# Scaling the last tile's rows on GpSimd, with the third placement and the last count moved, in a routed decoder trunk

## The chip, the cores and the metric

One core of a Trainium2 chip runs the whole program in one launch. The metric is the device time of that launch in microseconds. Three runs of the kernel before gave a median of 1433.36 us (1432.27 to 1435.67).

## What is computed

A decoder trunk of two layers over 512 rows of 1024 numbers (four tiles of 128 rows). Each layer runs a token mixer (gated convolution in layer 0, mLSTM in layer 1) beside a cross-attention, one output projection, a LayerNorm, and a mixture of 32 experts with a router. Cut to what the change touches:

```python
y = jnp.concatenate([h_loc, h_mem], axis=-1) @ w_out[i]
x = layer_norm(ALPHA * x + y, ln1_g[i], ln1_b[i])
scores = jax.nn.sigmoid(x @ router_w)
sel = (scores + router_b).reshape(n_tok, N_GROUPS, EXPERTS_PER_GROUP)
group_score = lax.top_k(sel, 2)[0].sum(-1)
_, g_idx = lax.top_k(group_score, 1)          # one group of four experts for each row
_, local = lax.top_k(in_group, 2)             # two experts in that group
counts = jax.ops.segment_sum(ones, e_flat)    # how many rows each expert gets
xb = x2[tok_buf]                              # the rows of each expert
```

After that each expert computes `(silu(x @ w_gate) * (x @ w_up)) @ w_down` on its rows.

## The kernel before, in words

All rows lie in on-chip memory as `x_sb[128, 4 tiles, 1024]`. `out_blocks` writes, for each layer, the end of the mixer and the routing; its parts `out_sp`, `out_pe`, `out_act` and `out_dve` are the instruction streams of SyncE, TensorE, ScalarE and VectorE, in the order written, tied by semaphores. The work goes tile by tile (t = 0 to 3).

VectorE's stream for tile t: `finish_sum` adds the projection to the residual (L872) and takes mean and variance (L879, L880). `place(t-1)` (L932 to L935) turns the counts of the tile before into positions, and writes `first_rows`, the 0/1 matrix that picks the rows of experts 0 and 1 (semaphore `first_marked`). `shift` subtracts the mean and multiplies by the gain (L886), then takes 1/std (L888, semaphore `inv_ready`). `scale` multiplies by 1/std and adds the bias (L893, semaphore `normed`). `scale_logits` scales the router's logits (L900), ScalarE makes the sigmoid of it (L833, semaphore `scored`), and `choose` (L909 to L926, twelve small instructions) finds the group and its two experts and writes `taken` (semaphore `chosen`). For tile 3 `scale` stands behind `scale_logits`. After tile 3 come `place(3)` and four pairs of a small reduction and a one-hot of 128x1024 (L978, L979, semaphore `marked`).

TensorE's stream: the projection of each tile (L703), transposes of its rows (`turn`, L727), the logits (`route`, L737), `count(t)` (L746), which needs `chosen` of tile t, and `pick_first(t, h)` (L760), which needs `first_marked` and `normed` of tile t and gathers by matmul the rows of experts 0 and 1, half h of the 1024 columns, into two banks over all four tiles. At the end, TensorE runs count(2), clears the banks, turn(3,1), pick(0,0), route(3,1), pick(0,1), pick(1,0), pick(1,1), pick(2,0), pick(2,1), count(3), pick(3,0), pick(3,1). ScalarE copies the two banks to `xgT` (L860) and sends tile 3's normalised rows to DRAM (L863, needs `normed` of tile 3). Then `gate_up(0)` (L1161) begins the experts. Inside it TensorE runs `code_rows` (L813, L816), which needs `marked` of all tiles.

The experts' weights come over SyncE's queue into nine places of `ring` (three 2 MB units for each expert, L170). Units 6, 7 and 8 are asked for when the last projection is done; unit n from 9 on is asked for when TensorE has finished reading the unit nine before it. GpSimd has nothing to do in the routing. It waits for `indexed`, for the stored rows and for the two picks, and then gathers the rows of the next experts (L1113); TensorE uses the first gather in `turn_rows(2)` (L1147), in the course of expert 1. Its way there is gate_up(0), gate_up(1), code_gates, turn_hidden(0), spread_ln (L1174, matmuls with one row), down(0) (L1209).

Of the kernel before, what the change touches and what calls it, by code (L numbers as in the profile page):

```python
# [9 lines left out]
ALU = mybir.AluOpType  # L10
# [23 lines left out]
TT = SEQ // P  # L34
# [18 lines left out]
class Chain:  # L53
# [10 lines left out]
    def then(self, ins):  # L64
        ins.then_inc(self.sem, 1)
        self.n += 1
        self.eng.wait_ge(self.sem, self.n)


def build_trunk(nc, x, xT_in, memT_in, conv_slabs, conv_qm, mlstm_w_in, smalls, w_kv_mem, w_out,  # L70
                ln1_g, ln1_b, ln2_g, ln2_b, w_pack, out):
    ctx = ExitStack()
    with ctx:
        phase_sems = []

        def sb(name, shape, dt=F32, at=ctx):
            return at.enter_context(nc.sbuf_tensor(name, shape, dt))

        def sem(name, at=ctx):
            if at is ctx:  # L80
                return ctx.enter_context(nc.semaphore(name))
            handle = nc.alloc_semaphore(name=name)
            phase_sems.append(handle)
            return handle
# [10 lines left out]
        x_sb = sb("x_sb", [P, TT, D_MODEL])  # L95
# [15 lines left out]
        stats, mv = sb("stats", [P, TT, 2, 6]), sb("mv", [P, TT, 4])  # L111
# [29 lines left out]
        dve_chain, act_chain, pool_chain = (Chain(sem(n)) for n in ("dve_chain", "act_chain", "pool_chain"))  # L141
# [504 lines left out]
        def out_blocks(l, ph, mem_l, pad, ln_rows, conv, xgT0, ln2_rows, xturned, xcopied, stored, indexed):  # L646
# [6 lines left out]
            ln_g, ln_b = ln_rows[:, 0:D_MODEL], ln_rows[:, D_MODEL:2 * D_MODEL]  # L653
# [13 lines left out]
            var_ready, std_ready, inv_ready, normed = s("var"), s("std"), s("inv"), s("normed")  # L667
# [31 lines left out]
            def out_pe(pe):  # L699
# [42 lines left out]
                def count(t):  # L742

                    pe.wait_ge(chosen, t + 1)
                    for q in range(t + 1):
                        last = nc.tensor.matmul(pos_of(t), before[:, :] if q == t else ones_bf[:, :],  # L746
                                                taken[:, q, :], start=(q == 0), stop=(q == t))
                    last.then_inc(counted, 1)
# [5 lines left out]
                def pick_first(t, h):  # L754

                    pe.wait_ge(first_marked, t + 1)
                    pe.wait_ge(normed, t + 1)
                    for c in range(4):
                        at = 512 * h + c * P
                        last = nc.tensor.matmul(FIRST_BANK[h][:, c * P:(c + 1) * P], x_sb[:, t, at:at + P],  # L760
                                                first_rows[:, t, :, :].rearrange("p j r -> p (j r)"),
                                                start=False, stop=(t == TT - 1 and c == 3))
                    if t == TT - 1:
                        last.then_inc(xturned, 1)
# [32 lines left out]
                pick_first(0, 0)  # L797
                route(TT - 1, 1)
                pick_first(0, 1)
                for t in (1, 2):  # L800
                    for h in range(2):
                        pick_first(t, h)
                count(TT - 1)
                for h in range(2):
                    pick_first(TT - 1, h)

# [59 lines left out]
            def out_dve(dve):  # L866
# [7 lines left out]
                def finish_sum(t):  # L874
                    xt, m = x_sb[:, t, :], mv[:, t, :]
                    dve.wait_ge(b_done, t + 1)
                    residual(bank[4 + t % 2], t, 1, summed)
                    dve.wait_ge(summed, t + 1)
                    then(V.bn_stats(stats[:, t, 1, :], xt[:, 512:1024]))  # L879
                    V.bn_aggr(m[:, 0:2], stats[:, t, :, :]).then_inc(var_ready, 1)  # L880
# [9 lines left out]
                def scale(t):  # L890
                    xt = x_sb[:, t, :]
                    dve.wait_ge(inv_ready, t + 1)
                    V.scalar_tensor_tensor(xt, xt, mv[:, t, 2:3], ln_b[:, :], ALU.mult, ALU.add).then_inc(normed, 1)  # L893
# [69 lines left out]
                dve.wait_ge(in_ln, 32)  # L963
                for t in range(TT):
                    finish_sum(t)
                    if t:
                        place(t - 1)
                    shift(t)
                    if t < TT - 1:
                        scale(t)  # L970
                    scale_logits(t)
                    if t == TT - 1:
                        scale(t)
                    choose(t)
                place(TT - 1)
                dve.wait_ge(first_marked, TT)
# [11 lines left out]
                then(V.tensor_reduce(most[:, 1:2], totals[:, N_EXPERTS:PICKED], AX.X, ALU.max))  # L988
                then(V.scalar_tensor_tensor(most[:, 2:3], most[:, 1:2], float(BLK - SLOTS), most[:, 0:1], ALU.add, ALU.max))
                then(V.tensor_copy(most_rows[0:1, 0:1], most[0:1, 2:3]))  # L990
            return out_sp, out_pe, code_rows, out_act, out_dve

        slabs = [(4 * MIX_W, 2 * ML_HEADS + XATT_W)] + [(512 * i, 512) for i in range(6)]
        by_k = lambda a: a[:, :].rearrange("p (k n) -> p k n", k=KT)
# [15 lines left out]
        def expert_phase(l, mem_l):  # L1010
# [3 lines left out]
            with ph:  # L1014
# [4 lines left out]
                ln_g, ln_b = flat[:, 2048:3072], flat[:, 3072:4096]  # L1019
# [6 lines left out]
                else:  # L1026
# [12 lines left out]
                combined, acc_read, var_ready, std_ready, normed, in_ln = (  # L1039
                    s("p2_" + n) for n in ("combined", "acc_read", "var", "std", "normed", "in_ln"))  # L1040
# [18 lines left out]
                later_sp, later_pool, later_pe, later_act, later_dve = later_blocks(  # L1059
                    l, ph, x1_rows, to_rows, ln_g, ln_b, scattered)  # L1060

                out_sp, out_pe, code_rows, out_act, out_dve = out_blocks(
                    l, ph, mem_l, pad, ln_rows, conv, xgT[0], (ln_g, ln_b), xturned, xcopied, stored, indexed)
                with nc.Block() as block:
                    @block.sync
# [42 lines left out]
                    @block.gpsimd  # L1108
                    def _(pool):
                        def gather(g):  # L1110
                            if g >= 3:
                                pool.wait_ge(scattered[g % 3], 16 * (g // 3))
                            nc.gpsimd.indirect_dma_start(xg[g % 3], None, x1_rows,  # L1113
                                                         bass.IndirectOffsetOnAxis(ap=tok_of_slot[:, g:g + 1], axis=0),
                                                         bounds_check=SEQ - 1, oob_is_err=False
                                                         ).then_inc(gathered[g % 3], 16)

                        if l == 0:
                            conv_pool(pool)
                        pool.wait_ge(indexed, 1)  # L1120
                        pool.wait_ge(stored, 16 * TT)
                        pool.wait_ge(xturned, 2)
                        for g in range(3):
                            gather(g)
                        for g in range(N_GROUPS):
                            pool.wait_ge(normed, g + 1)
                            nc.gpsimd.indirect_dma_start(to_rows,
                                                         bass.IndirectOffsetOnAxis(ap=tok_of_slot[:, g:g + 1], axis=0),
                                                         xg[g % 3], None, bounds_check=SEQ - 1, oob_is_err=False
                                                         ).then_inc(scattered[g % 3], 16)  # L1130
                            if g + 3 < N_GROUPS:
                                gather(g + 3)
                        later_pool(pool)
# [1201 lines left out]
```

## Time and profile before

| | us |
|---|---|
| median of 3 runs | 1433.36 |
| the profiled execution, its own time | 1435.61 |
| its span, first to last instruction | 1433.7 |
| TensorE matmul busy | 1350.4 (94%) |
| VectorE busy | 511.6 (36%) |
| ScalarE busy | 305.4 (21%) |
| GpSimd busy | 39.3 (3%) |

The routing of tile 3 and the picks lie at 198 to 209 us of the span in layer 0 and at 958 to 968 us in layer 1; the experts follow until about 665 us and 1425 us. In the page's slices the DMA engines are over 90% busy from 215 to 645 us and from 968 to 1398 us, at 413 to 428 GB/s. The page shows busy time, and the timelines show start and length of each instruction, with the idle time before it and what ended it in brackets. L12 is line 12 of the kernel before.

### The profile page before, as it was taken

What the parts mean: (1) busy time and instruction counts of PE and PEld (TensorE: products, weight loads), DVE (VectorE), ACT (ScalarE), POOL (GpSimd) and SP (SyncE); (2) the same over time, 40 slices, a digit from 0 to 9 for tenths busy, and PEclk for the clock granted to TensorE, in tenths of its full rate; (3) what the DMA queues carried; (4) which work ended last, traced back from release to release, by engine and by line L of the source; (5) the groups of instructions that cost most, each with busy time, mean ns of one, the idle gap of its engine ahead of it and who ended that gap; (6) DMA issues with size and microseconds to landing.
All of it is one profiled execution on the core that took longest, in us unless ns stands there. A gap on an engine that the chain in (4) does not pass through costs nothing. (4 is left out here: it accounts for less than half of the span.)

```text
span 1433.7 us, 16402 instructions
## 1 busy us (share of the span) xinstructions
PE 1350.4 (94%) x6686; PEld 719.5 (50%) x6688; DVE 511.6 (36%) x1046; ACT 305.4 (21%) x524; POOL 39.3 (3%) x64
## 2 busy tenths in 40 slices
PE   9999999999999898988899997899999999989885
PEld 7877873333333333324677886683333333333331
DVE  5365582123123122122634258583122122122121
ACT  5233331011011011011443135441011011010111
POOL 1000000000000000000000000000000000000000
PEclk9999999999999999999999999899999999999998
DMA  9320959999999999998131102859999999999994
GB/s 371 162 89 13 383 210 413 428 426 428 428 426 427 427 427 428 427 427 352 60 117 66 53 1 107 334 203 420 429 426 427 428 426 428 427 427 428 428 427 186
DMA packets 39492, 463.77 MB, mean 323 GB/s; under 512 B 6388, under 2 KB 6516, under 8 KB 12152
## 3 DMA queue, kind: packets, MB, share of 16 engines
q1 hardware_dynamic: 34520, 453.25, 75.5%
q0 software_dynamic: 4608, 8.40, 1.5%
q8 instruction: 55, 0.90, 0.3%
q10 hardware_dynamic: 288, 1.05, 0.2%
q14 instruction: 21, 0.17, 0.0%
HBM read 458.47 MB, written 12.58 MB: 329 GB/s over the span
## 5 line engine op out<-in xcount | busy, mean ns | idle before, releaser
L1161 PE MATMUL bank<-ring,xT 128*64 128x512 f32 x2048 | 462.1, 599 | 38.8 <-DMA ring<-in_w_pack 38.7
L1161 PEld LDWEIGHTS bank<-ring,xT 128*64 128x64 f32 x2048 | 148.2, 137 | 307.9 <-issue 307.6
L1209 PE MATMUL bank<-ring,pad 128*64 128x512 f32 x1024 | 236.0, 602 | 2.1 <-issue 1.1
L1403 DVE COPY xT<-bank 128x512 f32<-128x512 f32 x60 | 41.5, 692 | 437.4 <-PE bank L1147 437.4
L1209 PEld LDWEIGHTS bank<-ring,pad 128*64 128x64 f32 x1024 | 68.2, 137 | 161.0 <-issue 150.6
L1312 ACT ACTIVATE pad<-bank 128x256 f32<-128x256 f32 x64 | 24.6, 384 | 447.3 <-PE bank L1161 447.3
L1318 ACT COPY pad<-bank 128x512 f32<-128x512 f32 x64 | 37.5, 587 | 336.6 <-PE bank L1209 336.6
L1413 DVE COPY pad<-bank 128x256 f32<-128x256 f32 x64 | 27.1, 423 | 176.4 <-PE bank L1184 176.4
L1147 PEld LDWEIGHTS bank<-x_sb 128*128 128x128 f32 x480 | 58.1, 191 | 49.7 <-issue 46.2
L1226 PE MATMUL bank<-pad,x_sb 64*128 64x512 f32 x256 | 72.3, 641 | 1.4 <-ACT pad L1318 1.4
L1147 PE MATMUL bank<-x_sb 128*128 128x128 f32 x480 | 69.5, 288 | 1.0 <-DMA x_sb<-x_rows,tok_of_slot 1.0
L481 PE MATMUL bank<-x_half_hi,w_half_hi 128*128 128x512 f32 x160 | 63.2, 395 | 0.9 <-DVE x_half_lo L563 0.5
L481 PE MATMUL bank<-x_half_hi,w_half_lo 128*128 128x512 f32 x160 | 62.3, 389 | 0.0
L481 PE MATMUL bank<-x_half_lo,w_half_hi 128*128 128x512 f32 x160 | 62.3, 389 | 0.0
L703 PE MATMUL bank<-w_out_half_hi,heads_half_hi 128*128 128x512 f32 x128 | 53.1, 415 | 6.8 <-DVE heads_half_lo L942 6.8
L1846 PE MATMUL bank<-x_half_hi,w_half_hi 128*128 128x512 f32 (+1 forms) x120 | 48.1, 401 | 4.1 <-PEq L90 4.1
L703 PE MATMUL bank<-w_out_half_lo,heads_half_hi 128*128 128x512 f32 x128 | 50.8, 397 | 0.0
L703 PE MATMUL bank<-w_out_half_hi,heads_half_lo 128*128 128x512 f32 x128 | 50.7, 396 | 0.0
L1846 PE MATMUL bank<-x_half_lo,w_half_hi 128*128 128x512 f32 (+1 forms) x120 | 47.7, 397 | 0.0
L1846 PE MATMUL bank<-x_half_hi,w_half_lo 128*128 128x512 f32 (+1 forms) x120 | 47.6, 397 | 0.0
L1956 DVE TENSOR_TENSOR w_half_lo<-ring,w_half_hi 128x1024 fp32r<-128x1024 f32 x24 | 29.5, 1240 | 45.6 <-ACT w_half_hi L1928 45.6
L1407 DVE TENSOR_TENSOR pad<-pad,bank 128x256 f32<-128x256 f32 x64 | 26.3, 411 | 31.6 <-ACT pad L1312 31.6
(302 smaller groups left out, 1492.7 us busy)
## 6 DMA issues: line engine op xcount, KB each, us to landing
ring<-in_w_pack SPq DMA_DIRECT2D x190, 2048.0 KB, 30.1
ring<-in_mlstm_w_in SPq DMA_DIRECT2D x6, 2048.0 KB, 7.3
ring<-in_w_out SPq DMA_DIRECT2D x2, 4096.0 KB, 12.8
ring<-in_conv_slabs SPq DMA_DIRECT2D x5, 1536.0 KB, 12.3
ring<-in_w_kv_mem SPq DMA_DIRECT2D x2, 2048.0 KB, 27.9
ring<-in_w_pack SPq DMA_DIRECT2D x4, 1024.0 KB, 40.5
x_rows<-x_sb SPq DMA_DIRECT2D x6, 512.0 KB, 2.6
ring<-in_xT SPq DMA_DIRECT2D x4, 512.0 KB, 6.4
```

What stands on the lines that cost most here:

```text
L481: last = nc.tensor.matmul(o[:, :], w[:, k, :], xh[:, k, :], start=(k == 0 and w is w_hi and xh is x_hi), stop=(k == KT - 1 and w is w_lo))
L703: last = nc.tensor.matmul(o[:, :], a, b, start=(k == 0 and i == 0), stop=(k == KT - 1 and i == 2))
L1147: last = nc.tensor.matmul(o[:, c * P:(c + 1) * P], xg[g % 3][:, 512 * h + c * P:512 * h + (c + 1) * P], pick[g % 2][:, 2 * (q % 2):2 * (q ...
L1161: last = nc.tensor.matmul(GU_BANK[e % 2][64 * f:64 * f + 64, :], xgT[e // 2 % 2][:, 4 * h + c, 64 * (e % 2):64 * (e % 2) + 64], gu[:, c, f ...
L1209: last = nc.tensor.matmul(Y_BANK[e % 2][64 * n:64 * n + 64, :], hidT[e % 2][:, c, 64 * f:64 * f + 64], dn[:, f, c, 512 * n:512 * n + 512], ...
L1226: last = nc.tensor.matmul(ACC[n][:, :], gateT[e // 2 % 2][rows, e % 2, :], y[e % 2][rows, :], start=(j == 0), stop=(j == PER_GROUP - 1))
L1318: nc.scalar.copy(y[e % 2][:, :], Y_BANK[e % 2][:, :]).then_inc(y_copied, 1)
L1403: V.tensor_copy(xgT[q % 2][:, 4 * h:4 * h + 4, :], o[:, :].rearrange("p (c r) -> p c r", c=4)).then_inc(xcopied, 1)
L1407: V.tensor_tensor(hid[e % 2][:, :], hid[e % 2][:, :], GU_BANK[e % 2][:, 256:512], ALU.mult).then_inc(hid_done, 1)
L1413: V.tensor_copy(hidT[e % 2][:, :, :].rearrange("p c r -> p (c r)"), H_BANK[:, 0:256]).then_inc(hcopied, 1)
L1846: last = nc.tensor.matmul(bank[results[m][2]][0:cols_of, :], w[:, k, 0:cols_of], xh[:, k, :], start=(k == 0 and w is hi and xh is x_hi), s ...
L1956: last = V.tensor_tensor(of(lo), part, of(hi), ALU.subtract)
```

## The change

VectorE no longer scales tile 3's rows. GpSimd does it in two instructions, a multiply by the per-row 1/std and an add of the bias row, with a wait of its own between them; the second raises `normed`. `place(2)` moves from ahead of `shift(3)` to behind `scale_logits(3)`. TensorE's count(3) moves ahead of pick(2,1).

```diff
@@ out_pe
-                for t in (1, 2):
-                    for h in range(2):
-                        pick_first(t, h)
+                for t, h in ((1, 0), (1, 1), (2, 0)):
+                    pick_first(t, h)
                 count(TT - 1)
+                pick_first(2, 1)
                 for h in range(2):
                     pick_first(TT - 1, h)
@@ out_dve
                 for t in range(TT):
                     finish_sum(t)
-                    if t:
+                    if 0 < t < TT - 1:
                         place(t - 1)
                     shift(t)
                     if t < TT - 1:
                         scale(t)
                     scale_logits(t)
                     if t == TT - 1:
-                        scale(t)
+                        place(t - 1)
                     choose(t)
@@ out_blocks
-            return out_sp, out_pe, code_rows, out_act, out_dve
+
+            def out_pool(pool):
+
+                t = TT - 1
+                pool.wait_ge(inv_ready, TT)
+                xt = x_sb[:, t, :]
+                pool_chain.then(nc.gpsimd.tensor_scalar(xt, xt, mv[:, t, 2:3], None, ALU.mult))
+                nc.gpsimd.tensor_tensor(xt, xt, ln_b[:, :], ALU.add).then_inc(normed, 1)
+            return out_sp, out_pe, code_rows, out_act, out_dve, out_pool
@@ expert_phase, block.gpsimd
                         if l == 0:
                             conv_pool(pool)
+                        pool_chain.bind(pool)
+                        out_pool(pool)
                         pool.wait_ge(indexed, 1)
                         pool.wait_ge(stored, 16 * TT)
                         pool.wait_ge(xturned, 2)
```

## Rows read from the trace of the kernel before

**Rows 1.** The page, costliest groups: busy, mean ns, idle before and its releaser.

```profile
L1161 PE MATMUL bank<-ring,xT 128*64 128x512 f32 x2048 | 462.1, 599 | 38.8 <-DMA ring<-in_w_pack 38.7
```

**Rows 2.** Timeline of TensorE, layer 0: start, length (us), line, operands, idle before.

```profile
200.19 1.02 PE L737 MATMUL bank<-gw,pad 128*128 128x32 f32 x8
201.05 4.71 PE L760 MATMUL bank<-pad,x_sb 128*128 128x128 f32 x40
205.79 0.24 PE L746 MATMUL bank<-taken,ones_bf 128*128 128x40 bf16 x3
...
206.74 2.05 PE L760 MATMUL bank<-pad,x_sb 128*128 128x128 f32 x16 [0.68 <-DVE pad L934]
208.72 3.65 PE L1161 MATMUL bank<-ring,xT 128*64 128x512 f32 x16
...
231.52 1.16 PE L1147 MATMUL bank<-x_sb 128*128 128x128 f32 x8 [1.04 <-DMA x_sb<-x_rows,tok_of_slot]
...
236.46 8.66 PE L1161 MATMUL bank<-ring,xT 128*64 128x512 f32 x32
...
251.15 7.09 PE L1161 MATMUL bank<-ring,xT 128*64 128x512 f32 x32
```

**Rows 3.** Timeline of VectorE, layer 0, tile 3.

```profile
199.51 0.21 DVE L880 BATCH_NORM_AGGREGATE mv<-stats 128x2 f32<-128x12 f32 x1
199.64 0.14 DVE L932 SCALAR_TENSOR_TENSOR pos<-bank,taken 128x32 f32<-128x32 f32 x1
...
199.90 0.28 DVE L934 TENSOR_TENSOR pad<-pos,row_of_block 128x128 f32<-128x128 f32 x1
200.10 1.28 DVE L886 SCALAR_TENSOR_TENSOR x_sb<-x_sb,mv,ln_rows 128x1024 f32<-128x1024 f32 x1
201.30 0.16 DVE L888 RECIPROCAL mv<-mv 128x1 f32<-128x1 f32 x1
201.56 0.25 DVE L900 SCALAR_TENSOR_TENSOR logit<-bank,mv,shares 128x32 f32<-128x32 f32 x1
201.72 1.27 DVE L893 SCALAR_TENSOR_TENSOR x_sb<-x_sb,mv,ln_rows 128x1024 f32<-128x1024 f32 x1
202.92 0.18 DVE L909 TENSOR_TENSOR sel<-score,smalls_sb 128x32 f32<-128x32 f32 x1
...
203.79 0.29 DVE L915 TENSOR_REDUCE rank<-lead 128x32 f32<-128x128 f32 x1
...
205.55 0.18 DVE L924 SCALAR_TENSOR_TENSOR taken<-rank,gsum 128x32 bf16<-128x32 f32 x1
206.10 0.19 DVE L932 SCALAR_TENSOR_TENSOR pos<-bank,taken 128x32 f32<-128x32 f32 x1 [0.36 <-PE bank L746]
```

**Rows 4.** Timeline of ScalarE, layer 0: the sigmoid and tile 3's store.

```profile
201.84 0.23 ACT L833 ACTIVATE score<-logit 128x32 f32<-128x32 f32 x1 [0.26 <-DVE logit L900]
...
208.84 0.35 ACTq L863 DMA_DIRECT2D x_rows<-x_sb  x1
```

**Rows 5.** Timeline of TensorE, layer 1: the picks of tile 3.

```profile
966.30 2.05 PE L760 MATMUL bank<-pad,x_sb 128*128 128x128 f32 x16 [0.68 <-DVE pad L934]
```

**Rows 6.** Timeline of GpSimd, start of the mLSTM phase.

```profile
689.59 0.86 POOL L1805 TENSOR_SCALAR_AFFINE_SELECT row_sel<-row_sel 6x768 f32<-6x768 f32 x1 [0.16 <-POOL row_sel L1804]
```

**Rows 7.** Timeline of VectorE, the same stretch.

```profile
689.87 1.66 DVE L1956 TENSOR_TENSOR w_half_lo<-ring,w_half_hi 128x1024 fp32r<-128x1024 f32 x1 [2.73 <-ACT w_half_hi L1928]
```

**Rows 8.** All instances of line L1956, 680 to 740 us: ns min/median/max.

```profile
L1956 DVE TENSOR_TENSOR w_half_lo<-ring,w_half_hi x10: 1204/1226/1659, 689.9 to 739.4; 128x1024 fp32r<-128x1024 f32 x10
```

**Rows 9.** Busy time by stretch: PE, PEld, DVE, ACT, POOL, granted clock, DMA share, GB/s.

```profile
242.00:244.00 2.00, 2.00 (x12) 0.65 (x10) 0.00 (x0) 0.00 (x0) 0.00 (x0) 1.00 0.89 221
...
1002.00:1004.00 2.00, 2.00 (x12) 0.73 (x9) 0.00 (x0) 0.33 (x1) 0.00 (x0) 1.00 0.96 360
```

**Rows 10.** Timeline of TensorE, first matmul of layer 1's output projection.

```profile
901.24 0.80 PE L703 MATMUL bank<-w_out_half_hi,heads_half_hi 128*128 128x512 f32 x1 [5.24 <-DVE heads_half_lo L942]
```

**Rows 11.** Busy time by stretch, behind the idle stretch of rows 10 (columns as rows 9).

```profile
902.00:904.00 2.00, 2.00 (x7) 1.52 (x6) 2.00 (x4) 2.00 (x5) 0.00 (x0) 0.50 1.05 291
```

More of the change, by code:

```diff
@@ L1060, in expert_phase @@
                     l, ph, x1_rows, to_rows, ln_g, ln_b, scattered)
-                out_sp, out_pe, code_rows, out_act, out_dve = out_blocks(
+                out_sp, out_pe, code_rows, out_act, out_dve, out_pool = out_blocks(
                     l, ph, mem_l, pad, ln_rows, conv, xgT[0], (ln_g, ln_b), xturned, xcopied, stored, indexed)
```

## The prediction

> **What bounds the kernel now.** I read the costliest groups first. The matmuls of gate and up, L1161, waited 38.7 us in all for weights [rows 1]: in the later part of each expert phase the weight stream sets the pace. So the first question is what a microsecond at the routing is worth. The stream can only run on when TensorE frees a place of the ring, and the table by stretches shows where it ran dry for that reason: at 242 to 244 us it moved 221 GB/s against some 430 beside it, (430 - 221) / 430 x 2 = 1.0 us lost, in layer 1 at 1002 to 1004 us 360 GB/s, 0.3 us lost [rows 9]. TensorE's progress decides there, and whatever comes later stays later until the end. A TensorE that is late therefore costs its full lateness in both layers. One that is early gives only what ran dry: all of a gain of 0.7 us in layer 0, at most some 0.5 us in layer 1 (0.3, and 0.2 for smaller dips).
>
> Next the timelines about the last tile. TensorE does five picks in 4.71 us, 0.94 each, and comes to count(3) at 205.79 [rows 2]. VectorE's choice, its twelve instructions from 202.92 to 205.73, ends just then [rows 3]: the two arrive together, so a gain on one alone is worth nothing. After the count VectorE places tile 3 and TensorE idles 0.68 us before the last two picks at 206.74; the experts start at 208.72 [rows 2]. Layer 1 repeats this with the same 0.68 us [rows 5].
>
> **The change, part by part, in layer 0.**
>
> *place(2) moved.* Mean and variance end at 199.72, place(2) starts at 199.64 and shift at 200.10 [rows 3]. Without place(2) shift waits only for the variance and starts about 199.75, 0.35 us earlier, so 1/std is ready at 201.11 rather than 201.46. The logits of tile 3 end at 201.21 on TensorE [rows 2]; L900 starts at 201.26 rather than 201.56. The sigmoid follows 0.28 behind and takes 0.23 [rows 4], and is ready for VectorE at about 201.8. place(2), 0.46 us, fills that wait. Its `first_marked` comes a microsecond or two later; pick(2,0) waits for it, and TensorE gets there only at 201.05 + 3 x 0.94 = 203.9, so this costs nothing.
>
> *scale(3) leaves VectorE.* It takes 1.20 us from start to start (201.72 to 202.92) [rows 3]. With place(2) in its stead, choose would start at 201.42 + 0.46 = 201.88, 1.04 us earlier, and end at 204.69.
>
> *count(3) ahead of pick(2,1).* TensorE is there after four picks, 201.05 + 3.77 = 204.82. The count holds TensorE some 0.26 us, pick(2,1) 0.94, so the last picks start 1.20 us behind the count, where it was 0.95 before. Were nothing else to change, they would start at 204.82 + 1.20 = 206.02, a gain of 0.72 us.
>
> *GpSimd's two instructions.* No row shows either. Nothing else stands in its queue. The nearest row is a select over 768 elements with one operand, 0.86 us [rows 6], 1.12 ns an element: 1.15 us for the multiply over 1024. The add reads two operands. Its low end is the same 1.15 us, its high end one turn more for the second operand, 2.3 us, and 3.4 if the write takes another turn. I take 2.3, as the row has one operand read and each is 1024 elements. The Trainium skill (GPSIMD Engine Reference, Performance versus the Vector engine) measures 4497 ns for such an add over 2048 elements, which would make about 2.25 us here by estimate, so the sum would hardly change. From 201.25 the pair alone would end at 201.25 + 1.15 + 0.15 + 2.3 = 204.85, before the last picks want the rows at 206.02: hidden, with 1.2 us to spare.
>
> *Beside each other.* The trace has one place where GpSimd reads memory while VectorE works on two operands from it. The select runs from 689.59 to 690.45 [rows 6]. VectorE's subtraction starts at 689.87 and takes 1.66 us [rows 7], where the median of ten is 1.226 [rows 8]. It lost 0.43 of the 0.58 us they overlap; its end, 691.53, is 1.08 us after GpSimd's. So it stood until GpSimd had finished. I take this as the rule for the choice. The Trainium skill (SBUF — State Buffer, Who interferes with whom) says the same and speaks against the change: whichever starts first holds the shared port for its whole instruction, and VectorE instructions with two SBUF inputs need it against a GpSimd instruction that reads. By that rule the sum is the one below; without it, it is rival 1.
>
> The multiply runs 201.25 to 202.4. place(2) ends with the two-operand L934, which would start at 201.7: it stands until 202.4 and ends near 202.45. Behind it sel and the first lead (L909, L911) can pass while GpSimd signals to itself and starts its add, until about 202.9. Then the add has the port, for 2.2 us, to 205.1. The second lead (L913) stands, and ends at 205.25. What is left of choose, from L915 at 203.79 to 205.73, is 1.94 us [rows 3]: `chosen` at 207.2, against 205.73 before. The order hardly matters: should the add come in earlier or later, chosen is 207.2 to 207.8. TensorE, ready at 204.8, idles 2.4 us. Last picks: 207.2 + 0.06 + 1.20 = 208.5, **1.7 us later** than 206.74 (range 1.4 to 2.3).
>
> **The sum.** Layer 1: 1.7 us, passed on in full. Layer 0: tile 3's store [rows 4] and the gather behind it are later too, but TensorE had 1.04 us to spare there, waiting for the gather at 231.52 [rows 2]. The store took 10.3 us because it shared the engines with units 6 to 8; issued 1.7 us later, it meets less of them. I credit the whole 1.04: 0.7 us. Together 2.4.
>
> Then the clock. TensorE idles 2.4 us in each layer where it idled 0.68. After a gap of 5.24 us [rows 10] the granted clock was 0.50, the level of 1.2 GHz [rows 11]. After 1.04 us of idling among thin matmuls, 32 matmuls took 8.66 us, where the same 32 later took 7.09: 1.6 us for one such stretch [rows 2]. A gap of 2.4 us lies between the two; the clock may hold or fall, in either layer. Low end nothing, high end 3.2 us. Taking one fall in two, I add 1.4 us (a fall may partly lie in the gap itself). Sum: 2.4 + 1.4 = **+3.8 us**.
>
> The profiled execution took 1435.61 us, 2.25 above the median: it would become 1439.4, the median 1433.36 becomes 1437.1. About 0.2%, 2.9 us, is what a measurement of this kernel can tell from no change.
>
> **The rivals.**
>
> 1. *GpSimd works beside VectorE at no cost.* The last picks start 0.72 us earlier; layer 0 gives 0.7, layer 1 at most 0.5: 1.2 us, 1432.1. For it: only one row shows the contention, and there the operands were large. Against it: that row's end follows GpSimd's. This rival is not slower. It is complete where choose ends by 204.8, and the time turns from slower to faster where choose ends before 206.74 - 1.20 - 0.06 = 205.5, so where VectorE loses less than 0.8 us of its 1.04.
> 2. *The add is short.* At 1.15 us the port is free at 204.0; chosen 206.1, last picks 207.3, +0.6 in each layer, of which layer 0 swallows its part: +0.6 in all, 1434.0.
> 3. *The port costs as forecast and the clock stays up.* +2.4, 1435.8; with both clocks falling +5.6, 1439.
> 4. *The part does not do what it says: the rows come late.* With 3.4 us for the add and a late start, `normed` comes at 206.3, still ahead of the picks at 208.5. It adds only through the port: 1.1 us more in each layer, +6 in all.
>
> **How the numbers follow.** The forecast, one clock fall: 0.34. Port cost with no fall 0.22, with two 0.14. Short add 0.10. No contention 0.15. Long add 0.05. Slower by over 0.2%: the forecast but for its lower edge, two falls, the long add, and a share of the case without a fall: 0.54. Faster by over 0.2%: no mechanism gives 2.9 us; 0.03 for a clock that falls less often elsewhere. Within: 0.43. For 8 in 10 the range runs from just above rival 1, 1432.2 less its noise, 1431.9, to two falls with the late end of the port, 1440.2. The likeliest sign's own range is 1436.2 to 1440.2.
>
> **What would show it.** L913 or its neighbours at 1 to 2.5 us instead of 0.29, ending just after GpSimd's add; L934 of tile 2 drawn out beside the multiply; count(3) at about 207.3 counted from the same start, with some 2.4 us idle before it; a shorter wait before the first L1147 in layer 0; a half-clock stretch at the start of gate_up in one layer. If the twelve instructions keep their 0.19 to 0.29 us and start a microsecond earlier, the forecast is wrong and rival 1 holds. If GpSimd's add is near 1.2 us, rival 2.

## The result, and the profile after

The changed kernel is slower. Its first set of six runs gave a median of 1439.93 us (1437.21 to 1441.35) beside 1434.13 us (six runs) for the kernel before; the ratio is 1.0034, 95% interval 1.0020 to 1.0047. A second set, eleven runs beside 35 of the kernel before, gave 1438.06 us beside 1435.03 us: 1.0023 (1.0014 to 1.0033). The prediction was 3.8 us, the ratios make 4.9 and 3.3 us. The profiled execution took 1437.21 us, the fastest of its six, with a span of 1435.2 us. It is therefore read here for the lengths of single instructions, and the total is read from the ratios.

GpSimd in layer 0, in the timeline of the changed kernel (L997 is the multiply, L998 the add); the kernel before has no such instructions:

```profile
201.15 2.86 POOL L997 TENSOR_SCALAR x_sb<-x_sb,mv 128x1024 f32<-128x1024 f32 x1 [193.91 <-DVE mv L888]
204.09 2.34 POOL L998 TENSOR_TENSOR x_sb<-x_sb,ln_rows 128x1024 f32<-128x1024 f32 x1
```

The multiply shows 2.86 us, the add 2.34 (2.85 and 2.34 in layer 1).

VectorE, layer 0, tile 3, against [rows 3]:

```profile
201.19 0.25 DVE L900 SCALAR_TENSOR_TENSOR logit<-bank,mv,shares 128x32 f32<-128x32 f32 x1
...
201.66 0.75 DVE L934 TENSOR_TENSOR pad<-pos,row_of_block 128x128 f32<-128x128 f32 x1
202.33 0.18 DVE L909 TENSOR_TENSOR sel<-score,smalls_sb 128x32 f32<-128x32 f32 x1
202.54 0.29 DVE L911 TENSOR_TENSOR lead<-sel 128x128 f32<-128x128 f32 x1
202.87 0.29 DVE L913 TENSOR_TENSOR lead<-lead,ahead 128x128 f32<-128x128 f32 x1
...
204.16 2.30 DVE L919 SCALAR_TENSOR_TENSOR gfirst<-gsum,top,down_from 128x8 f32<-128x8 f32 x1
...
207.04 0.18 DVE L924 SCALAR_TENSOR_TENSOR taken<-rank,gsum 128x32 bf16<-128x32 f32 x1
```

The start is near what was computed: the logits at 201.19, and the choice (L909) at 202.33. In the text that follows an instruction that "stands" has begun but is held up, so that it is shown longer than it is elsewhere; what is called a hold is the time for which GpSimd keeps it so. Two instructions are drawn out. L934 takes 0.75 us where it took 0.28 [rows 3]; it ends at 202.41, 1.26 us after the multiply began. L919, of two operands and eight numbers each, takes 2.30 us where it takes 0.23 in tile 3's choice of the kernel before; it starts 0.07 us behind GpSimd's add and ends at 206.46, 0.03 us behind its end. Between them L909, L911 and L913, each with two operands, ran at their usual 0.18 and 0.29 us although the multiply was still shown as running. The choice ends at 207.22, against 205.73 [rows 3].

TensorE, layer 0, then layer 1, against [rows 2] and [rows 5]:

```profile
200.99 3.82 PE L760 MATMUL bank<-pad,x_sb 128*128 128x128 f32 x32
207.28 0.24 PE L746 MATMUL bank<-taken,ones_bf 128*128 128x40 bf16 x3 [2.47 <-DVE taken L924]
...
207.39 4.24 PE L760 MATMUL bank<-pad,x_sb 128*128 128x128 f32 x24
211.56 3.93 PE L1171 MATMUL bank<-ring,xT 128*64 128x512 f32 x16
...
966.70 0.28 PE L746 MATMUL bank<-taken,ones_bf 128*128 128x40 bf16 x3 [2.46 <-DVE taken L924]
...
966.84 4.39 PE L760 MATMUL bank<-pad,x_sb 128*128 128x128 f32 x24
971.16 3.65 PE L1171 MATMUL bank<-ring,xT 128*64 128x512 f32 x16
```

It idles 2.47 us ahead of count(3). Then 24 pick matmuls take 4.24 and 4.39 us; at 0.94 us for eight they would take about 2.9. The granted clock by stretch (columns as in [rows 9]) shows why:

```profile
209.00:212.00 3.00, 3.00 (x15) 2.63 (x15) 3.00 (x6) 0.92 (x2) 0.00 (x0) 0.50 1.01 431
967.00:969.50 2.50, 2.50 (x13) 2.50 (x13) 2.38 (x7) 0.00 (x0) 0.00 (x0) 0.50 1.01 433
```

The clock is at 0.50, the 1.2 GHz level, behind each gap. The experts start at 211.56, where it was 208.72 [rows 2]. In layer 0 the third expert's gate and up, 32 matmuls, and the fourth's follow at

```profile
238.40 7.09 PE L1171 MATMUL bank<-ring,xT 128*64 128x512 f32 x32
...
251.51 7.09 PE L1171 MATMUL bank<-ring,xT 128*64 128x512 f32 x32
```

against 236.46 (8.66 us long) and 251.15 in [rows 2].

Since executions drift by some tenths ahead of this place, the table counts from the start of the transposes of tile 3 (L727, 198.81 us in the trace of before, 198.74 in the changed one) to two events. The second column is the start of gate_up(0), the third the start of the last scaling in the expert phase (L1433 before); both are differences of starts in the timelines, layer 0 / layer 1.

| kernel (one execution each) | experts start | phase ends |
|---|---|---|
| before | 9.91 / 9.91 | 469.92 / 468.45 |
| changed | 12.82 / 12.99 | 470.48 / 470.12 |
| changed, second trace | 11.50 / 13.09 | 468.84 / 470.84 |

### The profile page after: what moved, and what is told of

The parts are those of the page before. It is cut to its first block and busy times, and to the rows that moved or that the text cites. A ratio compares the mean times of both kernels' runs of the same rounds, so it can differ in the third digit from the quotient of the medians.

```text
span 1435.2 us, 16406 instructions
## 1 busy us (share of the span) xinstructions
PE 1349.4 (94%) x6688; PEld 721.2 (50%) x6688; DVE 514.3 (36%) x1044; ACT 305.3 (21%) x524; POOL 50.2 (3%) x68
## 6 DMA issues: line engine op xcount, KB each, us to landing
ring<-in_conv_slabs SPq DMA_DIRECT2D x5, 1536.0 KB, 12.1
```

## Experiments

Twelve runs in three groups of four, each group on one chip beside runs of the kernel before: nine kernels, two of them twice, and the changed kernel again. The "experts' start" is counted as in the table, and "late" is against the kernel before, layer 0 / layer 1. The end of the choice is the end of L924. The first two undo one half of the change each.

**Only GpSimd.** The placement and the count go back; GpSimd scales.

```diff
-                    if 0 < t < TT - 1:
+                    if t:
...
-                    if t == TT - 1:
-                        place(t - 1)
...
-                for t, h in ((1, 0), (1, 1), (2, 0)):
-                    pick_first(t, h)
-                count(TT - 1)
-                pick_first(2, 1)
+                for t in (1, 2):
+                    for h in range(2):
+                        pick_first(t, h)
+                count(TT - 1)
```

> Only the scaling goes to GpSimd; place(2) and count(3) stand where they stood before. Port theory (VectorE instructions with two operands in SBUF stand while GpSimd reads): in choose(3) one instruction stands about 2.1 us beside the add and one about 0.5 us beside the multiply, the choice ends near 207.5 us, the experts start 1.8 us late or more in each layer, and the time is 3 to 6 us above before. Order theory (the lateness comes from the moved placement and count, GpSimd costs nothing): the twelve instructions keep 0.16 to 0.29 us, the choice ends near 204.9, and the time is within 1 us of before.

Measured: 1.0025 (1.0015 to 1.0034), 3.6 us. VectorE and GpSimd:

```profile
202.42 0.61 DVE L909 TENSOR_TENSOR sel<-score,smalls_sb 128x32 f32<-128x32 f32 x1 [0.29 <-ACT score L833]
...
205.14 2.05 DVE L922 TENSOR_SCALAR gsum<-down_from,top 128x8 f32<-128x8 f32 x1
```

```profile
201.87 2.86 POOL L995 TENSOR_SCALAR x_sb<-x_sb,mv 128x1024 f32<-128x1024 f32 x1 [194.72 <-DVE mv L888]
204.81 2.35 POOL L996 TENSOR_TENSOR x_sb<-x_sb,ln_rows 128x1024 f32<-128x1024 f32 x1
```

The port theory holds and the order theory falls. Now sel is the one that stands in the multiply's first part (0.61 us), and the one caught by the add is L922, 2.05 us. L922 has a single operand: I had spoken only of instructions with two. TensorE idled 1.46 us ahead of the count, and the clock did not fall behind that wait in either layer: the experts started at 11.34 / 11.35, 1.4 us late where 1.8 or more was expected.

**No GpSimd.** The placement and the count stay moved; VectorE scales.

```diff
                     if t == TT - 1:
                         place(t - 1)
+                        scale(t)
                     choose(t)
...
-                        out_pool(pool)
```

> place(2) and count(3) moved as in the change, but VectorE scales tile 3 itself ahead of the choice. Port theory: no instruction stands; the choice ends near 205.85, count(3) has 1 us of idle TensorE ahead of it, the last picks start 0.4 us late, 0.4 to 0.8 us in all, no clock fall there. Order theory: as late as the changed kernel, 2.8 us in each layer, 4 to 6 us in all.

Measured: 1.0007 (0.9996 to 1.0017), not to be told from before. No VectorE instruction stands; TensorE waits 1.12 us for the choice and the experts start 10.16 / 10.16, 0.25 us late (0.4 was expected for the last picks):

```profile
205.96 0.24 PE L746 MATMUL bank<-taken,ones_bf 128*128 128x40 bf16 x3 [1.12 <-DVE taken L924]
...
208.93 3.65 PE L1170 MATMUL bank<-ring,xT 128*64 128x512 f32 x16
```

The last picks are held by pick(2,1) behind the count, as the prediction's step on the count has it. The moved placement and count bring nothing by themselves, as far as this run can tell, and harm little.

**The choice waits for GpSimd.** This times GpSimd's two instructions with almost nothing beside them.

```diff
                         place(t - 1)
+                        dve.wait_ge(normed, TT)
                     choose(t)
```

> The changed kernel with VectorE waiting for tile 3's rows before it chooses, so nothing of VectorE runs beside GpSimd's add, and only place(2) beside the multiply. This measures GpSimd's two instructions by themselves. If the multiply's 2.86 us in the changed kernel were stretched by VectorE's two-operand instructions, it takes 1.2 to 1.6 us here and the choice ends near 208.2. If it is slow by itself, it takes 2.4 to 2.9 us here and the choice ends near 209.8. The add takes 2.3 us in both. The time is 1 to 3 us above the changed kernel.

Measured: 1.0060 (1.0045 to 1.0075), 8.6 us.

```profile
201.59 2.86 POOL L998 TENSOR_SCALAR x_sb<-x_sb,mv 128x1024 f32<-128x1024 f32 x1 [194.45 <-DVE mv L888]
204.53 2.34 POOL L999 TENSOR_TENSOR x_sb<-x_sb,ln_rows 128x1024 f32<-128x1024 f32 x1
```

```profile
202.10 0.75 DVE L934 TENSOR_TENSOR pad<-pos,row_of_block 128x128 f32<-128x128 f32 x1
206.91 0.19 DVE L909 TENSOR_TENSOR sel<-score,smalls_sb 128x32 f32<-128x32 f32 x1 [4.06 <-POOL x_sb L999]
```

The multiply is 2.86 us as well with only L934 beside it: it is slow by itself, and the choice does not stretch it. It keeps L934 from ending until 202.85, 1.26 us after its start, as before. The clock fell behind the 4.55 us gap in both layers, and the experts started 16.15 / 15.75, so 6.2 and 5.8 us late; the time grew by 8.6 of these 12.1 us, and that is 3.7 and 5.3 us above the two sets of the changed kernel, more than the 1 to 3 expected.

**One operand in GpSimd's second instruction.** The bias is left out for tile 3.

```diff
-                nc.gpsimd.tensor_tensor(xt, xt, ln_b[:, :], ALU.add).then_inc(normed, 1)
+                nc.gpsimd.tensor_scalar(xt, xt, eps_col[:, 0:1], None, ALU.add).then_inc(normed, 1)
```

> GpSimd's add of the bias row is replaced by the add of one number to each element, so its second instruction reads one operand; the bias is left out for tile 3. If the length of the stand goes by what GpSimd reads: the second instruction holds VectorE about 1.2 us at most, the choice ends at 206.0 to 206.4, and the gap of TensorE is near 1.3 us, short enough for the clock to hold. If VectorE stands as long as the GpSimd instruction lasts: it stands 2 us or more again, and the choice ends at 207 or later.

```profile
204.66 2.85 POOL L998 TENSOR_SCALAR x_sb<-x_sb,eps_col 128x1024 f32<-128x1024 f32 x1
```

```profile
204.72 1.07 DVE L919 SCALAR_TENSOR_TENSOR gfirst<-gsum,top,down_from 128x8 f32<-128x8 f32 x1
```

The second instruction is longer than the two-operand add, 2.85 us, and yet holds L919 only 1.07 us, until 205.79, 1.13 us after its own start. L922 and L923 then took their usual 0.23 and 0.17 us while GpSimd's instruction was still shown. So what VectorE stands for is not how long GpSimd's instruction is shown, but a part of it: the first 1.1 to 1.3 us with one operand of 1024 numbers, the whole with two. Why GpSimd's instruction lasts longer than it holds VectorE is not shown. The choice ended at 206.55; this execution ran 0.48 us behind that of before when tile 3's transposes began, so that is 206.07 on the scale of the expectation. The gap was 1.25 us, and the clock held. Time: 0.9998 (0.9987 to 1.0010).

**GpSimd in halves of 512 columns.**

```diff
+                xt = [x_sb[:, t, 512 * h:512 * h + 512] for h in range(2)]
+                nc.gpsimd.tensor_scalar(xt[0], xt[0], mv[:, t, 2:3], None, ALU.mult)
+                pool_chain.then(nc.gpsimd.tensor_scalar(xt[1], xt[1], mv[:, t, 2:3], None, ALU.mult))
+                nc.gpsimd.tensor_tensor(xt[0], xt[0], ln_b[:, 0:512], ALU.add)
+                nc.gpsimd.tensor_tensor(xt[1], xt[1], ln_b[:, 512:1024], ALU.add).then_inc(normed, 1)
```

> GpSimd multiplies and adds in halves of 512 columns. If its time goes by elements: multiplies of about 1.45 us each (2.86 for both), adds of about 1.2 us, one VectorE instruction stands about 0.5 us in the first multiply, another in the second, and one in each add for about 1 us. If the multiply has a tail that does not depend on its size (2.86 us, of which only the first 1.2 hold VectorE): each multiply takes some 2.2 us or the first is short and only the last, ahead of the wait, is long. The choice ends at 207.2 or a little earlier in the first case.

```profile
201.88 1.58 POOL L997 TENSOR_SCALAR x_sb<-x_sb,mv 128x512 f32<-128x512 f32 x1 [194.72 <-DVE mv L888]
203.44 1.56 POOL L998 TENSOR_SCALAR x_sb<-x_sb,mv 128x512 f32<-128x512 f32 x1
205.08 1.26 POOL L999 TENSOR_TENSOR x_sb<-x_sb,ln_rows 128x512 f32<-128x512 f32 x1
206.30 1.25 POOL L1000 TENSOR_TENSOR x_sb<-x_sb,ln_rows 128x512 f32<-128x512 f32 x1
```

```profile
205.07 1.29 DVE L922 TENSOR_SCALAR gsum<-down_from,top 128x8 f32<-128x8 f32 x1
206.40 1.19 DVE L923 CAST taken<-gsum 128x8 bf16<-128x8 f32 x1
```

GpSimd's time goes by elements (2 x 1.57, 2 x 1.26), and the second multiply starts 1.56 us behind the first, so the length shown is GpSimd's own pace. In the two multiplies L934 took 0.33 us and L916 0.34, so they stood 0.05 and 0.15 us, less than the 0.5 expected: each multiply of 512 columns held VectorE until 0.7 to 0.8 us after its start. Each add holds one instruction until its own end: L922 1.29 us, then L923, a cast of one operand that takes 0.17 us otherwise, 1.19 us. The gap was 2.21 us, the clock fell in both layers, the experts started 12.86 / 12.86. The ratio, 1.0017 (1.0005 to 1.0029), lies under the changed kernel's first one though the experts start as late: single sets are uncertain by over a microsecond.

**GpSimd writes only.** Fills in place of the two; tile 3 stays unscaled.

```diff
-                pool_chain.then(nc.gpsimd.tensor_scalar(xt, xt, mv[:, t, 2:3], None, ALU.mult))
-                nc.gpsimd.tensor_tensor(xt, xt, ln_b[:, :], ALU.add).then_inc(normed, 1)
+                flat = onehot[:, 0, :, :].rearrange("p g s -> p (g s)")
+                for i in range(3):
+                    pool_chain.then(nc.gpsimd.memset(flat, 0.0))
+                nc.gpsimd.memset(flat, 0.0).then_inc(normed, 1)
```

> GpSimd's two instructions are replaced by four that only write (fills of a tile that is not in use yet, some 4 to 5 us in all); tile 3's rows stay without the division by their deviation and without the bias, and VectorE waits for GpSimd only behind place(3). If reads of memory are what VectorE stands for: the twelve instructions and L934 keep their 0.16 to 0.29 us, the choice ends near 204.7, the experts start 0.5 to 0.8 us earlier than before in each layer, and the time is 0.5 to 1.5 us under before. If any GpSimd instruction holds VectorE: two or more instructions stand for about 1 us each and the choice ends at 206 or later.

```profile
201.68 2.98 POOL L999 MEMSET onehot<- 128x1024 bf16 x3 [194.39 <-DVE mv L888]
204.72 0.95 POOL L1000 MEMSET onehot<- 128x1024 bf16 x1
```

```profile
202.22 0.28 DVE L934 TENSOR_TENSOR pad<-pos,row_of_block 128x128 f32<-128x128 f32 x1
...
204.72 0.98 DVE L922 TENSOR_SCALAR gsum<-down_from,top 128x8 f32<-128x8 f32 x1
```

Neither line of the expectation came out whole. The two-operand instructions, L934 among them (L919 took its 0.23 us), ran at their usual lengths beside the fills: reads are what they stand for. But L922, with one operand, began together with the last fill, 0.95 us, and took 0.98. One instruction stood, the choice ended at 205.99 (205.5 with the 0.5 us taken off by which this execution ran behind) and most of the gain was gone: the experts started 9.71 / 9.70, 0.2 us early, ratio 1.0002 (0.9992 to 1.0012). So there are two kinds of stand: instructions with two operands against GpSimd's reads, and the one-operand L922 (fp32 in on-chip memory) against its writes. Whether writes alone would hold the cast L923 too is not shown; it stood beside an add, which reads and writes.

**VectorE late without GpSimd.** One more one-hot of 1.2 us ahead of the choice makes it as late as in the changed kernel.

```diff
                         place(t - 1)
+                        V.tensor_tensor(onehot[:, 0, :, :], slot1[:, 0, :].unsqueeze(2).broadcast_to([P, N_GROUPS, SLOTS]),
+                                        row1_of_slot[:, :].unsqueeze(1).broadcast_to([P, N_GROUPS, SLOTS]), ALU.is_equal)
+                        scale(t)
                     choose(t)
...
-                        out_pool(pool)
```

> GpSimd does nothing in the routing; VectorE scales tile 3 itself and runs one more two-operand instruction of 1.2 us (the one-hot of tile 0, written again later) ahead of the choice, so that the choice ends as late as in the changed kernel. Port theory: GpSimd harms only by making the choice late. Then no instruction stands, the choice ends near 207.1, TensorE idles 2.3 us ahead of count(3), the clock falls as in the changed kernel, and the time is that of the changed kernel within 1.5 us. If GpSimd's work costs something by another way (its own end, the store, the gathers), this kernel is 2 us or more faster than the changed one.

TensorE in layer 0, then in layer 1:

```profile
207.31 0.24 PE L746 MATMUL bank<-taken,ones_bf 128*128 128x40 bf16 x3 [2.27 <-DVE taken L924]
...
207.42 2.92 PE L760 MATMUL bank<-pad,x_sb 128*128 128x128 f32 x24
...
966.84 4.55 PE L760 MATMUL bank<-pad,x_sb 128*128 128x128 f32 x24
```

Measured: 1.0020 (1.0010 to 1.0029), beside 1.0023 (1.0014 to 1.0033) for the changed kernel on the same chip. The gap is 2.27 us. Against the expectation the clock fell only in layer 1 (4.55 us for the 24 picks) and held in layer 0 (2.92). GpSimd harms by making the choice late; another cost of it of 1.5 us or more would have shown as a faster kernel here, and did not.

**The gap filled.** Three matmuls of 128x512 stand ahead of count(3).

```diff
+                for _ in range(3):
+                    nc.tensor.matmul(T_BANK[0][:, :], ones_f[:, :], x_sb[:, 0, 0:512], start=True, stop=True)
                 count(TT - 1)
                 pick_first(2, 1)
```

> The changed kernel, with three more matmuls of 128x512 on TensorE ahead of count(3), into a bank that nobody reads then; they fill most of the 2.5 us in which TensorE waits for the choice. Clock theory (the half-clock stretch behind the wait is due to TensorE's own idling and costs some 1.2 to 1.6 us in each layer): the granted clock stays at 1.00 behind the picks, 24 pick matmuls take 2.9 us and not 4.2, and the time is 1.5 to 3 us under the changed kernel, that is 2 to 3.5 us above before. Without that theory: the clock falls as before and the time is that of the changed kernel or more.

The three are shown as six, and three picks as 24:

```profile
204.50 2.74 PE L803 MATMUL bank<-x_sb,ones_f 128*128 128x512 f32 x6
...
207.25 2.92 PE L760 MATMUL bank<-pad,x_sb 128*128 128x128 f32 x24
210.11 3.65 PE L1173 MATMUL bank<-ring,xT 128*64 128x512 f32 x16
```

The 24 picks take 2.92 us, the clock stays up there, and the experts start 11.51 / 11.50, 1.3 to 1.5 us earlier than in the changed kernel's first trace, with VectorE standing as long as ever (L919's counterpart 2.30 us). Time: 1.0016 (1.0005 to 1.0027). Because this interval touches the changed kernel's, I ran both again together.

> The changed kernel once more, on one chip with the three others, since the lateness of the experts' start in its first trace (2.9 and 3.1 us) is more than either layer was longer there (0.6 and 1.7 us). If the weight stream takes up part of the lateness, the time is again 4 to 6 us above before, with the experts' start 2.9 us late in each layer; a second trace also says whether the clock falls behind the gap each time.

> The changed kernel with TensorE's gap filled by three matmuls, once more, on one chip with the changed kernel. Clock theory: no fall behind the picks, experts' start 1.6 us late in each layer instead of 2.9, time 1 to 3 us under the changed kernel. Otherwise the same time as the changed kernel.

Measured on one chip: changed 1.0023 (1.0014 to 1.0033), 3.3 us where 4 to 6 were expected; filled 1.0010 (1.0000 to 1.0020), 1.9 us apart. The intervals still touch, but both sets have the same sign, and the second trace of the changed kernel shows the mechanism within one execution. Layer 0, then layer 1:

```profile
207.51 0.24 PE L746 MATMUL bank<-taken,ones_bf 128*128 128x40 bf16 x3 [2.47 <-DVE taken L924]
...
207.63 2.92 PE L760 MATMUL bank<-pad,x_sb 128*128 128x128 f32 x24
...
964.43 0.28 PE L746 MATMUL bank<-taken,ones_bf 128*128 128x40 bf16 x3 [2.47 <-DVE taken L924]
...
964.57 4.49 PE L760 MATMUL bank<-pad,x_sb 128*128 128x128 f32 x24
```

The gap is 2.47 us in both. In layer 0 the clock held, the picks took 2.92 us, and the experts started 11.50, 1.6 us late and not the 2.9 expected; in layer 1 it fell, 4.49 us, and they started 13.09. A fall costs 1.6 us here.

**Two halves on VectorE.** No GpSimd; the first half stands between the choice and place(3), the second behind it.

```diff
+                def scale_half(t, n):
+                    half = x_sb[:, t, n * 512:(n + 1) * 512]
+                    dve.wait_ge(inv_ready, t + 1)
+                    V.scalar_tensor_tensor(half, half, mv[:, t, 2:3], ln_b[:, n * 512:(n + 1) * 512],
+                                           ALU.mult, ALU.add).then_inc(normed, 1)
...
                     choose(t)
+                scale_half(TT - 1, 0)
                 place(TT - 1)
+                scale_half(TT - 1, 1)
...
-                    pe.wait_ge(normed, t + 1)
+                    pe.wait_ge(normed, t + 1 + (h if t == TT - 1 else 0))
...
-                act.wait_ge(normed, TT)
+                act.wait_ge(normed, TT + 1)
...
-                        out_pool(pool)
```

> No GpSimd. place(2) and count(3) as in the change; VectorE scales tile 3 in two halves of 512 columns, one between the choice and place(3), one behind place(3), and each last pick waits for its own half. Port theory: nothing stands, the choice ends near 204.7, the last picks start near 206.1 to 206.4, 0.4 to 0.7 us earlier than before in each layer, and the time is 0.5 to 1.3 us under before. Order theory: still late by 2 us or more in each layer.

> No GpSimd, tile 3 scaled in two halves on VectorE behind the choice, once more. The experts' start is 0.77 us early in each layer; what reaches the end is at most 1.5 us, 0.1%, so 0.3 to 1.5 us under before and 4 us or more under the changed kernel.

```profile
204.96 0.24 PE L746 MATMUL bank<-taken,ones_bf 128*128 128x40 bf16 x3
...
205.07 3.10 PE L760 MATMUL bank<-pad,x_sb 128*128 128x128 f32 x24
208.10 3.65 PE L1176 MATMUL bank<-ring,xT 128*64 128x512 f32 x16
```

No gap is left: count(3) follows the fourth pick at once, and the picks and the experts follow it. The experts start 9.14 / 9.14 in the first trace and 9.14 / 9.13 in the second, 0.77 us early in each layer. The times are 0.9995 (0.9985 to 1.0005) and 0.9992 (0.9982 to 1.0003): 0.7 and 1.1 us under before, of the size expected, but both intervals include no change, so no gain over the kernel before is shown. Against the changed kernel on the same chip it is 4.5 us faster (1433.57 against 1438.06), and the two intervals do not touch.

## Why the prediction was right

*What bounds.* The two engines do meet at count(3): 0.77 us off both of them came through to the experts' start as 0.77 (two halves), while VectorE's lateness came through in full where it was alone (only GpSimd: choice 1.4 us late, experts 1.4). That this lateness then counts in full to the end in both layers is wrong. The first trace of the changed kernel has phases 0.56 and 1.67 us longer for starts 2.9 and 3.1 us late, its second -1.1 and +2.4; the two traces of the halves on VectorE, which start alike, end layer 0 at 470.26 and 467.78. The trace shows where it goes. In layer 0 of the changed kernel TensorE is 2.91 us late at the experts' start, 2.0 at the third expert's gate and up (238.40, against 236.46 [rows 2], each from tile 3's transposes) and 0.43 at the fourth's (251.51 against 251.15); in the second trace it is 1.59 us late, 0.4 late, and 1.2 early. The two traces of the halves are 0.2 and 1.2 us early at that last place. In layer 1 3.08 us late stays 3.08.

The weights' queue says the same. Counted packet by packet from the start of tile 3's transposes, it is behind that of before, from 40 MB on and without change until 185 MB, by 0.8 us in layer 0 and 2.7 in layer 1 (first trace), -0.1 and 2.8 (second), and by 4.3 and 4.8 in the kernel whose choice waits: 3.5, 2.7 and 9.1 us in all. The phase ends are blurred besides by half clock near the end: at 640 to 645 us the trace of before has a granted clock of 0.74. In the times, 12.1 us of late starts gave 8.6 (the choice that waits), and 4.8 to 6.0 us gave 3.3 to 4.9 (the change). The stream's own loss shows in the table by stretch: in layer 0 it no longer ran dry at 242 us but lost its time earlier (323 GB/s at 216 to 220 us, 436 before), in layer 1 it ran dry for longer than in [rows 9]:

```profile
242.00:244.00 2.00, 2.00 (x12) 0.60 (x10) 0.00 (x0) 0.00 (x0) 0.00 (x0) 1.00 1.00 410
1002.00:1004.00 2.00, 2.00 (x12) 0.71 (x10) 0.00 (x0) 0.00 (x0) 0.00 (x0) 1.00 0.67 287
1004.00:1006.00 2.00, 2.00 (x12) 0.57 (x8) 0.00 (x0) 0.00 (x0) 0.00 (x0) 1.00 1.01 254
```

*place(2), scale(3), count(3).* Right to 0.1 us. In the halves kernel, where nothing stands, the choice ends at 204.89 in an execution that ran 0.15 us behind (204.69 was said), and the experts start 3.14 us behind the count, where the prediction's 1.20 and two picks of 0.99 make 3.18.

*GpSimd's durations.* The add was right, 2.34 us for 2.3. The multiply was mis-sized: 1.15 us was scaled from the select's row [rows 6], and it takes 2.86. Hence the sentence that the pair would end at 204.85 and be hidden with 1.2 us to spare is wrong: it ended at 206.43, after the 206.02 at which the last picks would have wanted the rows. Even with no contention the change could have gained at most about 0.3 us in each layer (206.43 against the 206.74 at which the last picks started before), and rival 1's 1.2 us was out of its reach.

*Beside each other.* `chosen` was said to come at 207.2 and came at 207.22, by another split. L934 stood 0.47 us as said. Then the longer multiply let seven instructions of the choice pass, and the add caught the eighth, L919, and not L913. As both the hold of the multiply (1.1 to 1.3 us) and that of the add (its whole length) are as they were taken, the sum is the same: 204.69 + 0.47 + 2.07 = 207.2. The right end time was partly luck: a stand of the length of 2.86 us in the multiply would have made it 1.6 us later. The prediction also named two-operand instructions alone; L922 and L923 stand too. The Trainium skill (SBUF — State Buffer, Who interferes with whom) has both kinds, and the traces agree on which pairs meet. They differ from it on one point: it says that the first holds the port for its whole instruction, and a one-operand GpSimd instruction of 2.86 us let VectorE's two-operand instructions through after 1.1 to 1.3 us. The measurement decides.

*The clock.* One fall in two layers was said, for 1.4 us; the term was too small. Of the gaps ahead of count(3), or of the last picks in the kernel before, those of 4.55 us fell in both layers; those of 2.2 to 2.5 us fell in six layers out of eight (the change's two traces, the halves on GpSimd, the late choice); those of 1.5 us and less in none of ten (the rest have no gap there). Each fall costs 1.3 to 1.6 us at the experts' start. At six in eight the term should have been 2 to 2.4 us. Why it falls in one layer and not in the other with the same gap is not shown. The prediction also laid the half clock of the kernel before behind 236 us (32 matmuls in 8.66 us; granted clock 0.57 at 236 to 240 us) to the 1.04 us of idling there. But such a fall needs no idling: in layer 1 of the same trace TensorE is busy throughout 980 to 990 us, and the granted clock is 0.72 at 985 to 990. Among the small matmuls of the first two experts such a stretch of half clock stands in 17 of the 28 layers traced.

*Layer 0's credit.* The wait for the gather, 1.04 us, is indeed gone: `turn_rows` starts without a wait in the changed kernel, and tile 3's store took 6.9 and 8.0 us in its two traces where the one of before took 10.8. But the credit was too small. In both traces of the changed kernel the half clock at 236 us is gone from layer 0 too, and the 32 matmuls behind it take 7.09 us instead of 8.66: another 1.6 us that layer 0 gets back. By the weights' queue it swallows 2.1 of its 2.91 us in the first trace and all of its 1.59 in the second. Whether the later start keeps the clock up there, or chance does, is not shown: the kernel with VectorE late, 1.38 us late in layer 0, has it too (0.57 at 236 to 240 us), with TensorE busy throughout the four microseconds ahead of it.

*The sum.* The port's part, 1.7 us a layer, is the 1.59 us that the second trace has in layer 0 with no fall (11.50 against 9.91), and 1.43 in the only-GpSimd kernel. 3.8 us in all lies between the two sets' 3.3 and 4.9. It does so by two errors that offset each other: the falls behind the gap cost 2.8 us in the first trace and 1.6 in the second, at the experts' start, where 1.4 was added; and what the two layers together swallow is 2.5 and 2.1 us where 1.04 was taken off (the weights' queue, 3.5 and 2.7 us behind in all, against 6.0 and 4.8 at the experts' start). So the agreement to a microsecond is in part luck, though the port, the wait at count(3) and the clock are as forecast in kind. Rival 1 is out (the reads do hold VectorE), rival 2 is out (the add is 2.34), rival 4 is out as to the add, though the pair's end was nearer to mattering than it said.

## What to carry to other kernels

Work handed to an idle engine is not free where one engine holds the other up at the memory, as GpSimd did VectorE here: look for what runs beside it, instruction by instruction, and count a stand for every pair that meets. On a path where two engines arrive together, a wait that is added to one delays in full what follows, and more than that where the clock falls behind it, as it did behind six of eight gaps of 2.2 to 2.5 us here. How much of the delay reaches the end is another question, and to be read layer by layer: follow one later instruction, such as the fourth expert's first matmul, and the weights' queue. And before moving work off an engine, see whether its pieces fit into waits that this engine already has: two halves of the same instruction on VectorE opened the path that GpSimd blocked.

## What was not expected

- GpSimd's multiply with one operand (128x1024 fp32) takes 2.86 us and its two-operand add 2.34 us: the instruction with fewer operands is the longer one, alone or beside others.
- The one-operand instruction holds VectorE for only the first 1.1 to 1.3 of its 2.86 us; the two-operand one for all 2.34.
- A fill on GpSimd, which reads nothing, holds a one-operand VectorE instruction of eight columns for 0.75 us (0.98 instead of 0.23).
- Two executions of the same program, with gaps of 2.46 to 2.47 us in every layer, had half clock behind the gap in both layers in one case and in a single layer in the other.
- Of a start 2.91 us late, layer 0 had 0.43 us left at the fourth expert's start, because a wait and a stretch at half clock that it had before were gone; layer 1, 3.08 us late, got nothing back.
